# A fourth unit of seven products in one pair of projection blocks, with the token sums moved five slots later

## The reference

```python
x += 0.5 * swiglu(rmsnorm(x), w_gate, w_up, w_down)          # 2048 -> 5504 -> 2048
proj = rmsnorm(x) @ w_in                                     # 2048 columns in, split into:
cq, ckv, kpe, hq, hf, hi, hg = jnp.split(proj, IN_SPLITS, axis=-1)
a = mla_group(cq, ckv, kpe, ...)                             # latent attention, 8 heads
r = hgrn2_group(hq, hf, hi, hg, lb, out_norm)                # gated linear recurrence, 8 heads
x += concat(a, r) @ w_out
x += memory_xattn(rmsnorm(x), rmsnorm(mem), ...)             # 4 heads, 256 memory tokens
x += 0.5 * swiglu(rmsnorm(x), ...)                           # a second one
```

```python
f = lb + (1 - lb) * sigmoid(fx); b = cumsum(log(f)); k = 1 - f
o_t = sum over s <= t of (q_t . (k_s * exp(b_t - b_s))) v_s
```

## Time and profile before

| | before |
|---|---|
| median of 3 runs | 1884.99 us (1883.53 to 1885.43) |
| the profiled execution's own time | 1883.42 us |
| its span, first to last instruction | 1881.6 us |
| TensorE busy | 1874.3 us |
| VectorE busy | 1599.2 us |
| ScalarE busy | 1094.7 us |
| GpSimd busy | 93.5 us |
| mean granted TensorE clock | 1.000 |

### The profile page before, as it was taken

How to read it: one execution, slowest core, us unless ns; L and a number is a source line. 1 busy time by engine, 2 the same in 40 slices (tenths; PEclk the granted TensorE clock), 3 DMA queues, 4 the chain that set the end, 5 groups by cost and what they waited for, 6 DMA issues and landing times.

```text
span 1881.6 us, 23322 instructions
## 1 busy us (share of the span) xinstructions
PE 1874.3 (100%) x8811; PEld 1571.3 (84%) x8811; DVE 1599.2 (85%) x2060; ACT 1094.7 (58%) x1487; POOL 93.5 (5%) x98
## 2 busy tenths in 40 slices
PE   9999999999999999999999999999999999999999
PEld 7888888888889888888888888888888888888987
DVE  6999999989999867786676764789999999999986
ACT  7665555555656547556476655656555555555553
POOL 0000000000000001302250000000000000000000
PEclk9999999999999999999999999999999999999999
DMA  9666555656556665455443654455655566655654
GB/s 338 224 197 200 195 197 195 224 202 201 180 186 213 217 227 155 148 190 191 136 156 112 212 190 135 156 187 195 200 188 194 201 207 216 202 198 183 196 193 172
DMA packets 176689, 362.58 MB, mean 193 GB/s; under 512 B 8512, under 2 KB 19776, under 8 KB 175936
## 3 DMA queue, kind: packets, MB, share of 16 engines
q1 hardware_dynamic: 176144, 360.89, 57.5%
q10 hardware_dynamic: 432, 0.19, 0.0%
HBM read 358.95 MB, written 2.10 MB: 192 GB/s over the span
## 4 chain that ended last, share of the span: by engine, by line
PE 94%; DVE 4%; issue 1%; ACT 0%; DMA 0%; POOL 0%; DVEq 0%; SPq 0%; ACTq 0%
PE acc L2087 18%; PE acc L2089 18%; PE acc L2088 18%; PE acc L2076 8%; PE acc L2078 8%; PE acc L2077 8%; PE small L2087 2%; PE small L2089 2%; PE small L2088 2%; DVE w_lo L1374 2%; PE tr L2035 2%; PE small L2288 1%; PE tr L2089 1%; PE tr L2087 1%; PE tr L2088 1%; PE tr L2103 1%
## 5 line engine op out<-in xcount | busy, mean ns | idle before, releaser
L1374 DVE TENSOR_TENSOR w_lo<-w_raw,w_hi 128x1024 fp32r<-128x1024 f32 (+3 forms) x776 | 757.7, 1030 | 55.5 <-ACT w_hi L764 43.3
L764 ACT ACTIVATE w_hi<-w_raw 128x1024 fp32r<-128x1024 f32 (+4 forms) x562 | 499.5, 924 | 135.9 <-PE acc L2089 104.6
L2087 PE MATMUL acc<-w_hi,hT_hi 128*128 128x512 f32 (+1 forms) x966 | 373.2, 386 | 0.0
L2089 PE MATMUL acc<-w_lo,hT_hi 128*128 128x512 f32 (+1 forms) x966 | 371.3, 384 | 0.0
L2088 PE MATMUL acc<-w_hi,hT_lo 128*128 128x512 f32 (+1 forms) x966 | 371.0, 384 | 0.0
L869 ACT ACTIVATE w_hi<-w_raw 128x1024 fp32r<-128x1024 f32 (+1 forms) x190 | 196.7, 1045 | 123.8 <-DVE w_raw L1362 74.6
L1303 DVE TENSOR_TENSOR w_lo<-w_raw,w_hi 128x1024 fp32r<-128x1024 f32 (+1 forms) x166 | 198.9, 1239 | 31.8 <-ACT w_hi L764 30.4
L2087 PEld LDWEIGHTS acc<-w_hi,hT_hi 128*128 128x128 f32 x966 | 181.4, 188 | 34.4 <-DVE w_lo L1374 0.5
L2089 PEld LDWEIGHTS acc<-w_lo,hT_hi 128*128 128x128 f32 x966 | 181.3, 188 | 34.4
L2088 PEld LDWEIGHTS acc<-w_hi,hT_lo 128*128 128x128 f32 x966 | 181.5, 188 | 33.6
L862 ACT ACTIVATE w_hi<-w_raw 128x512 fp32r<-128x512 f32 (+3 forms) x190 | 154.1, 831 | 91.9 <-PE acc L2089 89.6
(11 more groups left out here) (344 smaller groups left out, 2611.4 us busy)
## 6 DMA issues: line engine op xcount, KB each, us to landing
w_raw<-in_ffn_w_down SPq DMA_DIRECT2D x56, 768.0 KB, 4.6
w_raw<-in_ffn_w_down SPq DMA_DIRECT2D x40, 1024.0 KB, 5.2
w_raw<-in_w_in SPq DMA_DIRECT2D x30, 1024.0 KB, 5.1
w_raw<-in_ffn_w_gate SPq DMA_DIRECT2D x58, 512.0 KB, 3.9
w_raw<-in_ffn_w_gate SPq DMA_DIRECT2D x38, 768.0 KB, 4.3
w_raw<-in_ffn_w_up SPq DMA_DIRECT2D x38, 768.0 KB, 4.6
w_raw<-in_ffn_w_up SPq DMA_DIRECT2D x54, 512.0 KB, 4.7
w_raw<-in_ffn_w_up SPq DMA_DIRECT2D x26, 1024.0 KB, 6.0
```

What stands on the lines that cost most here:

```text
L764: nc.scalar.activation(piece(w_hi, c % SPLIT, k0, k1, width), piece(raw, c % RAW, k0, k1, width), ACT.Copy).then_inc(hi_done, 1)
L1374: v.tensor_tensor(piece(w_lo, c % RAW, k0, k1, width), piece(raw, c % RAW, k0, k1, width), piece(w_hi, c % SPLIT, k0, k1, width).bitcast(F ...
L2087: mm(dst, lhs_hi, wh, start=first, stop=False)
L2089: return mm(dst, lhs_hi, wl, start=False, stop=last)
```

## The change

The pair gets four units in place of three, the tiles 6 and 7 of the rows going from a plain slot to the new unit, and its plain slots have two tiles each (four of hf1, four of hq1) where they had four, three and three. The sums of activations become four groups; they are made on VectorE behind the low parts of slots 15 to 18 in place of 10 to 12, their high parts by ScalarE in slots 16 to 19, and split in slots 17 to 19 and inside the pair's first unit. Their tiles move to other places. TensorE waits for the sums of each unit at that unit. The first two plain slots of hq1, two tiles each, stand ahead of the transposes of hf1, where one of four tiles did. VectorE takes the queries behind slot 28 in place of 29, and makes the running sums behind slot 29 in place of 28.

```diff
@@ tiles
-        mS_hi = at("mS_hi", A0 + 44, [P, 3, 4, P], F32R)
-        mS_flat = at("mS_flat", A0 + 50, [P, 2, SEQ])
-        mS_lo = at("mS_lo", A0 + 68.5, [P, 3, 4, P], F32R)
-        mS_sum = at("mS_sum", A0 + 68.5, [P, 3, 4, P])
+        mS_hi = at("mS_hi", A0 + 44, [P, 4, 4, P], F32R)
+        mS_flat = at("mS_flat", A0 + 36, [P, 2, SEQ])
+        mS_lo = at("mS_lo", A0 + 66.5, [P, 4, 4, P], F32R)
+        mS_sum = at("mS_sum", A0 + 66.5, [P, 4, 4, P])
@@ the plan
-        number(slots, "mix", 4 * len(MIX) + 4)
+        number(slots, "mix", 4 * len(MIX) + 8)
-        PAIR = Duo(0, True, 0, 0, NW, "upupup", [0, 2, 4], [(6, 4), (10, 3), (13, 3)])
+        PAIR = Duo(0, True, 0, 0, NW, "upupupup", [0, 2, 4, 6], [(8, 2), (10, 2), (12, 2), (14, 2)])
-            return M + m if m < 4 * MB else M + m + 4
+            return M + m if m < 4 * MB else M + m + 8
+        short += PAIR.firsts + PAIR.seconds
@@ ScalarE, mixer(m)
-                if m in (11, 12, 13):
-                    act.wait_ge(ev("mix_sums_made"), m - 10)
-                    nc.scalar.activation(mS_hi[:, m - 11], mS_sum[:, m - 11], ACT.Copy).then_inc(ev("mix_sums_hi"), 1)
+                if m in (16, 17, 18, 19):
+                    act.wait_ge(ev("mix_sums_made"), m - 15)
+                    nc.scalar.activation(mS_hi[:, m - 16], mS_sum[:, m - 16], ACT.Copy).then_inc(ev("mix_sums_hi"), 1)
@@ ScalarE, pair()
                 hi(PAIR.seconds[1], 0, PAIR.plains[1][1], NW)
+                hi(PAIR.seconds[2], 0, PAIR.plains[2][1], NW)
                 for t in range(TT):
...
-                hi(PAIR.seconds[2], 0, PAIR.plains[2][1], NW)
+                hi(PAIR.seconds[3], 0, PAIR.plains[3][1], NW)
@@ VectorE
+            def split_sums(n):
+
+                dve.wait_ge(ev("mix_sums_hi"), n + 1)
+                v.tensor_tensor(mS_lo[:, n], mS_sum[:, n], mS_hi[:, n].bitcast(F32), ALU.subtract).then_inc(ev("mix_sums_split"), 1)
@@ VectorE, pair()
                     if n == 0:
                         step_take(STEPS - 1)
+                        split_sums(3)
...
-                lo_parts(PAIR.seconds[2], PLAIN_PARTS[PAIR.plains[2][1]], NW)
+                for n in (2, 3):
+                    lo_parts(PAIR.seconds[n], PLAIN_PARTS[PAIR.plains[n][1]], NW)
@@ VectorE, mixer(m)
-                if m in (10, 11, 12):
-                    n = m - 10
+                if m in (15, 16, 17, 18):
+                    n = m - 15
...
-                if m in (12, 13, 14):
-                    n = m - 12
-                    dve.wait_ge(ev("mix_sums_hi"), n + 1)
-                    v.tensor_tensor(mS_lo[:, n], mS_sum[:, n], mS_hi[:, n].bitcast(F32), ALU.subtract).then_inc(ev("mix_sums_split"), 1)
-                for h, m0 in ((0, 6), (1, 27)):
+                if m in (17, 18, 19):
+                    split_sums(m - 17)
+                if m == 28:
+                    queries_taken()
+                for h, m0 in ((0, 6), (1, 28)):
...
-                if m == 29:
-                    queries_taken()
@@ TensorE, pair_unit(n)
+                pe.wait_ge(ev("mix_sums_split"), n + 1)
                 if first:
-                    pe.wait_ge(ev("mix_sums_split"), len(PAIR.raws))
@@ TensorE, pair()
                 pair_plain(1, 0)
+                pair_plain(1, 1)
                 pe.wait_ge(ev("forgets_scaled"), 1)
                 turn_features(groups["hf1"], 0, of(gate))
-                pair_plain(1, 1)
                 pair_plain(1, 2)
+                pair_plain(1, 3)
```

## The result

The changed kernel takes 1888.61 us (18 executions, 1888.1 to 1891.97), the kernel before 1883.82 beside it (18, 1883.2 to 1886.12): ratio 1.0024, 95% interval 1.0018 to 1.0031. It is slower by 4.8 us, as forecast; the number was 1890.8, 2.2 too high. The profiled execution took 1888.54 us, 5.12 more than that of before.

A forecast was written before the change was run, and what follows sets the result against it. TensorE, busy 1874.3 of 1881.6 us, was taken as the bound. Late takes 6.2, product -0.68 and restart 0.3 gave +5.8 us, moving the median from 1884.99 to 1890.8; range 1886.0 to 1893.0.

The forecast's parts named there:

- Takes in VectorE's laps: Slots 15 to 18: sums and splits ahead of VectorE's takes from `small` make TensorE's steps late, 6.2 us in all.
- four waits: TensorE waits for AT at the steps of slots 14, 15, 16 and 17, some 6 us more in all.
- Contention: VectorE's two-SBUF-operand sums take turns with GpSimd, about 1.0 us of each GpSimd row inserted in VectorE's stream.
- rival 1: Slots 15 to 18: sums slip in beside GpSimd, steps late by only 2.7; +2.3 us, 1887.3; chance 0.22.
- the condition that I had set: The forecast is wrong if the sum rows (mS_flat) show 0.69 us each beside running GpSimd rows.
- The pair: Fourth unit saves one product, -0.68 us; the restarted accumulator's wait for saved parts adds 0.3; VectorE's low parts cost nothing.
- The product: In the pair, the fourth unit drops one product of three matmuls on TensorE: -0.68 us.
- the restart: In the pair, TensorE restarts an accumulator before VectorE has saved P5 to P7: 0.3 us with the signal.
- rival 3: VectorE becomes the bound in the pair too, 1 to 2 us more: 1892 to 1893; chance 0.08.
- The base: Median of the runs shown before the change, 1884.99 us, to which the forecast +5.8 us was added.
- Queries ahead of the running sums: After the pair, VectorE reaches the running sums about a slot later: nothing; without cover, some 2 us.

The follow-up runs named there:

- e1: The changed kernel with its token sums put back to slots 10 to 13, splits to 12 to 14 and the pair: 1883.39 us, ratio 0.9998.
- e2: The kernel before with only its three token sums moved to slots 15 to 17, splits to 17 to 19: 1887.54 us, ratio 1.0021.
- e3: The changed kernel with sums and splits in the same slots but behind the take and the waves' products on VectorE: 1888.09 us, ratio 1.0022.
- e9: e4 with both tiles of the first token half ahead of the accumulator's restart in the pair: 1881.28 us, ratio 0.9986.
- e8: e5 with the take of slot 19 ahead of its low parts as well: 1886.27 us, ratio 1.0012.
- e10: e1 with the take ahead of the low parts in slot 16 alone: 1881.71 us, ratio 0.9988.
- e5: The changed kernel, sums still late, with takes ahead of low parts and sums in slots 15 to 18: 1889.25 us, ratio 1.003.
- e6: e1 with one group of four sums moved from slot 13 to slot 15: 1885.94 us, ratio 1.001.
- e4: e1 with the takes of slots 15, 16 and 17 ahead of their low parts: 1881.85 us, ratio 0.999.
- e11: The kernel before, its sums and three units unchanged, with takes of slots 15 to 17 ahead of the low parts: 1882.03 us, ratio 0.999.

## Why the prediction was right, and by how much its terms were off

**Takes in VectorE's laps** (+6.2 forecast, +5.12 measured at the pair's start in the profile). The mechanism held: what stood ahead of the takes made the steps late (2.3, 3.7, 4.3 and 6.2 forecast; 1.7, 2.9, 4.5 and 5.1 measured), and what was late after the pair was late at its start. e1 and e2 show it from both sides. Two details were otherwise. I expected four waits with some 6 us more in all; there were three, with 4.4 in all (1.76, 2.32, 0.35) where before there was one of 1.2. And the step of slot 16, for which I had a wait, had none: by its take (795.73) it could have started at 796.30, 3.4 late, and the lower clock made it 4.5. That this lies so near to 4.3 is luck. The size of the term was about 1 us too high: slot 15's sums ended at 779.32, not at 779.92, of which 0.46 is that VectorE reached this slot's low parts earlier (774.25, before 774.71), with no split left in slot 14: I had put the sums' going from the early slots at nothing. From there each lap was a little shorter than its sum of rows. Low parts and sums of slot 16 took 5.83 (781.65 to 787.48; forecast 5.87), but take and products ahead of them 2.33, not 2.5; in slot 18 low parts, sums, split and ckvT_lo took 7.03, not 7.27.

**Contention.** The sum rows took 1.52 to 1.55 where they began beside a running GpSimd row, 0.69 in e1, with none beside them, and 0.68 or 0.69 in e3, where none ran when they began. (The Trainium skill, SBUF — State Buffer, section "Who interferes with whom", has it that a VectorE instruction with two SBUF inputs and a GpSimd one that reads SBUF exclude each other; the trace agrees: all four sum rows lost 0.83 to 0.86.) That rules out rival 1 by the condition that I had set, and the time, 1888.6, is also above its 1887.3. The 1.0 us that I took for each GpSimd row was a little high: the row of six pieces in the earlier trace rows has two half ones, not one, which makes 1.14 for a whole piece, and (4.08 - 2.28) / 2 = 0.9 for a row. Rival 1's own sum was off too: the walk with one row of 1.0 us less in each lap ends at some 2.1 late, not 2.7, which makes it 1886.7.

**The pair** (-0.68 + 0.3 = -0.38 forecast; -0.29 measured, to the first matmul of slot 29 48.74 us before, from 815.50 to 864.24, 48.45 after). The product was right; the restart cost 0.40 (e9), not 0.3. VectorE was no bound in the pair of the changed kernel: rival 3 falls. It came in sight in e8, a wait of 0.66.

**The base.** The three executions shown of before had a median of 1884.99; 18 give 1883.8. Two of the three (1884.99 and 1885.43) lie in the upper of the two levels that the last section tells of. That is 1.2 of the 2.2 us of the miss; the over-sized laps are the rest.

**What I hadn't seen** is the clock. In the changed kernel it fell in slot 16, and by the rows it costs less than the 1.6 us that it adds there. VectorE worked without a wait from 776.70 to the take at 804.63, on which the step of slot 17 hangs, so that step would have come near 805.2 in any case; a faster slot 16 would have waited longer. The executions don't contradict it: the four at a mean clock of 0.998 took 1888.1 to 1888.6, the thirteen at 0.999 from 1888.3 to 1891.1; the longest, 1891.97, is the one at 0.997. But none of the 18 shows 1.000. That no clock loss at all would leave the changed kernel's time as it is, is argued from this and not shown: no kernel was made whose TensorE stays busy through the waits.

In e3 the share of the clock stays open. Its profile has 3.24 of some 4.6 us in the stretch with the low clock, and VectorE stood idle there 1.34 us for ScalarE. On the other side, the take for the step of slot 18 starts at 811.26 and the step at 812.04, 0.2 us more than the 0.57 between them, so VectorE was late there too; and one execution at a mean of 1.000 took 1887.92, within the range of the others.

Queries ahead of the running sums were costed at nothing: after the pair no wait for them shows in any of these profiles. They were not run alone.

## What to carry to other kernels

Work that is free because an engine is 85% busy is free only where that engine has a lead: read the lead at each place (here the start of a take against the step that needs it) before moving work there. The same 1.8 us cost nothing in slots 10 to 13 and 17, and 2.5 us in slot 15. Putting the instruction that is waited for ahead of the bulk work wins a wait back at no cost (1.7 us here, e10 against e1, by one take), but not once the laps as a whole are longer than the bottleneck's.

## What the runs showed of the hardware

A short wait of TensorE can be followed by a halved clock. In each profile with a wait for AT of 1.38 us or more (the changed kernel, e2, e3, e5, e6, e8) the granted clock fell to 0.50 for 3.4 or 6.8 us: in e5 during the wait of 4.24, in the others 0.5 to 2.3 us behind its end. It doesn't always: in the changed kernel it fell behind the second wait (2.32) and not behind the first (1.76), and in e6 two of eleven executions, in e8 eight of ten, show a mean clock of 1.000. The 1.2 us of the kernel before were enough in some of its executions: 23 of 90 have a mean clock of 0.999 and take 1884.8 to 1886.1, where all but two of the other 67 lie between 1883.1 and 1884.3. The kernels without the wait (e4, e9, e10, e11) show a mean of 1.000 in all of 43 executions, and each of them spreads over 1.1 us at most. Removing a wait of 1.2 us so also removed the second level of the time. In all these kernels the short matmuls of a step (16 of 64 columns) stand right behind the wait; whether they have a part in the fall was not tried.
